# Gate and up projections of a SwiGLU FFN as 2x2 block products, three of eight K steps in Strassen's seven products (float32 in two halves, one core)

## The reference

```python
hf = rmsnorm(x, norm_ffn[l])
act = jax.nn.silu(jnp.einsum('bsd,df->bsf', hf, w_gate[l])) * jnp.einsum('bsd,df->bsf', hf, w_up[l])
x = x + jnp.einsum('bsf,fd->bsd', act, w_down[l])
return rmsnorm(x, norm_final)
```

## Time and profile before

| what | value |
|---|---|
| median of 3 runs | 1759.29 us (1758.98 to 1760.27) |
| profiled execution, span from its first to its last instruction | 1757.6 us |
| median of the runs over that span | 1.7 us |
| TensorE busy | 1745.9 us, 99% |
| VectorE busy | 862.1 us, 49% |
| ScalarE busy | 747.8 us, 43% |
| HBM read, mean rate | 328 MB, 188 GB/s |
| mean granted TensorE clock | 0.998 of full |

### The profile page before, as it was taken

The page is one execution under the profiler, slowest core; times in us unless marked ns, Lnnn a source line. Parts: engine busy times, 40 slices in busy tenths (PEclk is TensorE's granted clock), DMA queues, the critical chain, the costliest instruction groups (busy, mean ns, idle before and its releaser), DMA issues.

```text
span 1757.6 us, 20453 instructions
## 1 busy us (share of the span) xinstructions
PE 1745.9 (99%) x7883; PEld 1448.9 (82%) x7883; DVE 862.1 (49%) x652; ACT 747.8 (43%) x655; POOL 33.2 (2%) x43
## 2 busy tenths in 40 slices
PE   9999999999999999999999999999999999999997
PEld 8888888888888888888888888888888888888886
DVE  5454455556565444444445554444444444444445
ACT  6444444445454433333333443433333333444444
POOL 1000010100000000000000000000000000000000
PEclk9999999999999999999999999999999999999999
DMA  8656655556555655655556565555555555555552
GB/s 284 195 172 191 190 165 172 167 168 184 164 177 191 198 195 187 195 187 194 187 197 228 190 217 190 187 187 187 186 188 181 191 185 189 207 191 191 191 192 94
DMA packets 150699, 331.11 MB, mean 188 GB/s; under 512 B 7328, under 2 KB 7424, under 8 KB 144640
## 3 DMA queue, kind: packets, MB, share of 16 engines
q1 hardware_dynamic: 150656, 330.50, 57.1%
HBM read 328.38 MB, written 2.10 MB: 188 GB/s over the span
## 4 chain that ended last, share of the span: by engine, by line
PE 99%; ACT 0%; DVE 0%; DMA 0%; POOL 0%; SPq 0%; issue 0%; DVEq 0%; POOLq 0%
PE ps L1132 27%; PE ps L1133 27%; PE ps L1141 27%; PE ps L1408 4%; PE ps L1401 4%; PE ps L1403 4%; PE ps L1150 2%; ACT sq_y L738 0%; PE ps L1230 0%; PE ps L1222 0%; PE ps L1240 0%; PE ps L1247 0%; PE ps L1246 0%; PE ps L1239 0%; DMA vec_rows<-in_conv_w 0%; PE ps L1232 0%
## 5 line engine op out<-in xcount | busy, mean ns | idle before, releaser
L755 DVE TENSOR_TENSOR w_lo<-w_raw,w_hi 128x2048 fp32r<-128x2048 f32 x308 | 707.3, 2299 | 653.4 <-ACT w_hi L424 651.2
L424 ACT ACTIVATE w_hi<-w_raw 128x2048 fp32r<-128x2048 f32 (+1 forms) x309 | 589.7, 1912 | 515.2 <-PE ps L1133 366.5
L1132 PE MATMUL ps<-w_hi,xT_hi 128*128 128x512 f32 x1024 | 404.5, 395 | 0.0
L1133 PE MATMUL ps<-w_hi,xT_lo 128*128 128x512 f32 x1024 | 398.7, 389 | 0.0
L1132 PE MATMUL ps<-w_hi,fT_hi 128*128 128x512 f32 x704 | 274.9, 391 | 0.0
L1133 PE MATMUL ps<-w_hi,fT_lo 128*128 128x512 f32 x704 | 274.0, 389 | 0.0
L1141 PE MATMUL ps<-w_lo,xT_hi 128*128 128x512 f32 x1024 | 253.0, 389 | 0.0
L1132 PEld LDWEIGHTS ps<-w_hi,xT_hi 128*128 128x128 f32 x1024 | 192.3, 188 | 39.9 <-issue 0.2
L1141 PEld LDWEIGHTS ps<-w_lo,xT_hi 128*128 128x128 f32 x1024 | 192.2, 188 | 39.9
L1133 PEld LDWEIGHTS ps<-w_hi,xT_lo 128*128 128x128 f32 x1024 | 192.3, 188 | 39.0
L1141 PE MATMUL ps<-w_lo,fT_hi 128*128 128x512 f32 x704 | 173.9, 389 | 0.0
(11 more groups left out here) (179 smaller groups left out, 1039.1 us busy)
## 6 DMA issues: line engine op xcount, KB each, us to landing
w_raw<-in_w_in SPq DMA_DIRECT2D x127, 1024.0 KB, 5.5
w_raw<-in_w_gate SPq DMA_DIRECT2D x44, 1024.0 KB, 5.2
w_raw<-in_w_up SPq DMA_DIRECT2D x44, 1024.0 KB, 5.2
w_raw<-in_w_down SPq DMA_DIRECT2D x44, 1024.0 KB, 4.8
w_raw<-in_w_branch_a SPq DMA_DIRECT2D x16, 1024.0 KB, 5.1
w_raw<-in_w_branch_b SPq DMA_DIRECT2D x16, 1024.0 KB, 5.0
w_raw<-in_w_out SPq DMA_DIRECT2D x16, 1024.0 KB, 5.1
xn<-in_x SPq DMA_DIRECT2D x4, 512.0 KB, 8.4
```

Of the source, the lines that this page charges most:

```text
L424: copy = lambda o, i, **kw: nc.scalar.activation(o, i, ACT.Copy, **kw)
L755: V.tensor_tensor(w_lo[:, chunk.split, :], w_raw[:, chunk.raw, :], w_hi[:, chunk.split, :].bitcast(F32), ALU.subtract).then_inc(lo_split, 1)
L1132: T.matmul(ps[:, banks + r, :], rows(hi, k, r), w, start=(q == 0 and k == 0), stop=False)
L1133: last = T.matmul(ps[:, banks + r, :], rows(lo, k, r), w, start=False, stop=False)
```

## The change

The gate and the up block of one turn are taken as one problem of 2x2 blocks. The rows of A are the two row tiles (256 tokens), its columns the two halves of K (K tiles c and c+8); the columns of B are gate and up. A step now loads K tile c and K tile c+8 of both gate and up, two DMAs of 512 KB for one of 1 MB, in the order `PAIR_OF`. Five of the eight steps ("s" in `STEPS`) do the eight plain block products. Three ("S") do Strassen's seven: they need sums of the weight blocks and sums of the activation tiles. All go into seven PSUM banks whose contents VectorE adds up at the end of the turn; the plain steps use the same banks, with the difference A1 - A2 (`D1`, `D2`) where a bank's result is used in both rows.

In an S step VectorE makes three sums of weight blocks from `w_raw` (`t_raw`, one operation of 1024 columns, two of 512), ScalarE makes `t_hi` (1536 columns), VectorE makes `t_lo` (1536 columns), and then both split the loaded block as before. One of the four loaded blocks is overwritten by a sum in place. The sums of the activation tiles (`form_hi`, `form_lo`, 22 tiles) are made once, in the last block of the output projection (`forms(0)`) and in the first FFN turn (`forms(1)`); for them the transposed block goes to `f_raw` first. At the end of a turn VectorE does seven additions of 512 columns (`u_step`, `c_step`) where there were none, ScalarE copies one bank out (`p1_out`), and silu is two separate operations. The product is transposed in two halves, behind steps 1 and 2. The first and last step of a turn run bank by bank and want both halves of their weights at the start.

```diff
+STEPS = "SssSsSss"
+PAIR_OF = (0, 2, 3, 1, 5, 4, 6, 7)
+LAST_S = 5
+B_P1, B_P6, B_P2, B_Q3, B_Q4, B_FREE, B_P7, B_Q5 = range(8)
...
+            def load_pair(i):
+                for j in range(2 * BC):
+                    c = Chunk(G_FFN + j, i, 2 * BC)
+                    sp.wait_ge(lo_split, c.count(1 - RAW_SLOTS))
+                    for u, w in ((1, w_gate_k), (0, w_up_k)):
+                        sp.dma_start(raw_units[:, c.raw, :, u, :],
+                                     halves(w)[:, :, PAIR_OF[j], bass.ds(i * COLS, COLS)]).then_inc(
+                                         pair_landed[c.raw], 16)
...
+            def pair_split(j, i):
+
+                c = Chunk(G_FFN + j, i, 2 * BC)
+                if STEPS[j] == "s":
+                    split(c, (pair_landed[c.raw], 32 * (j // RAW_SLOTS + 1) + i * 64))
+                    return
+                before = S_BEFORE[j] + i * S_TURNS
+                act.wait_ge(t_step, before * T_STEPS + T_STEPS)
+                if not (starts(i) and j == 0):
+                    last = max(k for k in range(-2 * BC, j) if STEPS[k] == "S")
+                    act.wait_ge(lo_used, Chunk(G_FFN + last, i, 2 * BC).count(1))
+                copy(t_hi[:], t_raw[:].rearrange("p u n -> p (u n)")).then_inc(t_hi_done, 1)
+                split(c, (t_step, before * T_STEPS + T_STEPS))
...
+                    dve.wait_ge(t_lo_done, before)
+                V.tensor_tensor(t_raw[:, 0:2, :], raw[:, 0:1, :].to_broadcast([P, 2, COLS]), raw[:, 1:3, :],
+                                ALU.add).then_inc(t_step, 1)
+                dve.wait_ge(t_step, before * T_STEPS + 1)
+                V.tensor_tensor(raw[:, 0, :], t_raw[:, 0, :], raw[:, 2, :], ALU.add).then_inc(t_step, 1)
+                dve.wait_ge(t_step, before * T_STEPS + 2)
+                V.tensor_tensor(t_raw[:, 2, :], raw[:, 0, :], raw[:, 3, :], ALU.add).then_inc(t_step, 1)
+                dve.wait_ge(t_hi_done, before + 1)
+                V.tensor_tensor(t_lo[:], t_raw[:].rearrange("p u n -> p (u n)"), t_hi[:].bitcast(F32),
+                                ALU.subtract).then_inc(t_lo_done, 1)
+                split(c)
...
+                    if j == LAST_S:
+                        dve.wait_ge(p1_out, i + 1)
+                        if not first:
+                            dve.wait_ge(act_turned, i * 2)
+                        V.tensor_tensor(c_up[:, 0, :], ps[:, B_P6, :], c_gate[:, 0, :], ALU.add).then_inc(u_step, 1)
+                        dve.wait_ge(u_step, i * 2 + 1)
+                        V.tensor_tensor(c_gate[:, 1, :], ps[:, B_P7, :], c_up[:, 0, :], ALU.add).then_inc(u_step, 1)
...
+                add(1, c_gate[:, 0, :], B_P2, c_gate[:, 0, :], ALU.add)
+                dve.wait_ge(u_step, i * 2 + 2)
+                add(2, c_up[:, 0, :], B_Q5, c_up[:, 0, :], ALU.subtract)
+                add(2, c_up[:, 1, :], B_Q5, c_gate[:, 1, :], ALU.subtract)
+                dve.wait_ge(c_step, i * 5 + 2)
+                add(3, c_up[:, 0, :], B_Q3, c_up[:, 0, :], ALU.add)
+                add(4, c_gate[:, 1, :], B_Q4, c_gate[:, 1, :], ALU.add)
...
+            SUMS = ((B_P1, "A11", 1), (B_P6, "S2", 0), (B_P7, "D1", 5), (B_P2, "A12", 3), (B_Q5, "S1", 4),
+                    (B_Q3, "S4", 2), (B_Q4, "A22", 6))
+            PLAIN = ((B_P2, "A11", 1), (B_P2, "A12", 3), (B_Q5, "A21", 0), (B_Q5, "A22", 2),
+                     (B_Q3, "D1", 0), (B_Q3, "D2", 2), (B_Q4, "A21", 1), (B_Q4, "A22", 3))
...
+                if 0 < j < 2 * BC - 1:
+                    for part in parts:
+                        last = high(part, False)
+                    last.then_inc(hi_used, 1)
+                    pe.wait_ge(lo_split, c.count(1))
+                    for n, part in enumerate(parts):
+                        last = low(part, final(part[0]) and part[0] not in [p[0] for p in parts[n + 1:]])
+                    last.then_inc(lo_used, 1)
+                    return
+                pe.wait_ge(lo_split, c.count(1))
```

More of the change, by code:

```diff
@@ L276, in hybrid_block, with units @@
         GRP_HM, GRP_M, GRP_F = 0, NB, 2 * NB
-        HI_HM, HI_M, HI_F = 0, NB * KB, NB * KB + NB
+        HI_HM, HI_M = 0, NB * KB
+        S_TURNS = STEPS.count("S")
+        S_BEFORE = [STEPS[:j].count("S") for j in range(2 * BC)]
+        T_STEPS = 3
+        F_BLOCKS = NB - 1
+        def units(half):
+            w = w_hi if half == 0 else w_lo
+            return w[:].rearrange("p s (u n) -> p s u n", u=4)
         @block.sync
@@ L688, in ffn_turn, with silu @@
+            def silu(i, r):
+                if starts(i):
+                    act.wait_ge(x1_rstd, 1)
+                act.wait_ge(c_step, (1, 5)[r] + i * 5)
+                nc.scalar.activation(c_gate[:, r, :], c_gate[:, r, :], ACT.Silu,
+                                     scale=r_x[:, 1, r:r + 1]).then_inc(silu_done, 1)
+            def ffn_turn(i, last=False):
                 first = starts(i)
                 for j in range(2 * BC):
[L690 removed]
@@ L695, in ffn_turn @@
                         else:
[L696 to L701, removed]
-                            act.wait_ge(dve_out, V_FFN + i)
-                        for r in range(RT):
-                            last = nc.scalar.activation(gate[:, r, :], ps[:, r, :], ACT.Silu, scale=r_x[:, 1, r:r + 1])
-                        last.then_inc(act_out, 1)
+                            silu(i - 1, 1)
@@ new lines, in ffn_turn @@
+                    if not first and j in (1, 2):
+                        act_taken(i - 1, j - 1)
+                    if first and j == 2:
+                        forms_high(1, form_raw1, 12, 10)
+                    if j == LAST_S:
+                        act.wait_ge(lo_used, Chunk(G_FFN + j, i, 2 * BC).count(1))
+                        if not first:
+                            act.wait_ge(dve_out, V_FFN + i)
+                        copy(c_gate[:, 0, :], ps[:, B_P1, :]).then_inc(p1_out, 1)
@@ L708, in stage @@
+                    if last and j == LAST_S + 1:
+                        stage(Chunk(G_DOWN))
+                    if j == 2 * BC - 1:
+                        silu(i, 0)
             def stage(chunk):
@@ new lines, in ffn_turn, with add @@
+                    if last and j == LAST_S + 1:
+                        stage(Chunk(G_DOWN))
+                def add(n, out, bank, in1, op):
+                    if n < 4:
+                        dve.wait_ge(bank_done, i * 3 + n)
+                    else:
+                        dve.wait_ge(lo_used, Chunk(G_FFN + 2 * BC - 1, i, 2 * BC).count(1))
+                    V.tensor_tensor(out, ps[:, bank, :], in1, op).then_inc(c_step, 1)
+                add(1, c_gate[:, 0, :], B_P2, c_gate[:, 0, :], ALU.add)
@@ new lines, in turn_half, with turn_act @@
+            def turn_half(source, h, done):
+                for k in range(2):
+                    for r in range(RT):
+                        last = T.transpose(ps[:, B_FREE, k * SEQ + r * P:k * SEQ + (r + 1) * P],
+                                           source[:, r, (2 * h + k) * P:(2 * h + k + 1) * P], ident[:])
+                last.then_inc(done, 1)
+            def turn_act(d, h):
+                pe.wait_ge(dve_out, V_FFN + 1 + d)
+                if not (starts(d) and h == 0):
+                    pe.wait_ge(act_out_of, d * 2 + h)
+                turn_half(c_up, h, act_turned)
```

341 lines of the change are left out of this document (245 added, 96 removed).

## The result

The changed kernel takes **1813.4 us** (median of four runs, 1812.3 to 1814.3), the kernel before 1759.1 beside it: the ratio is 1.031, with a 95% interval of 1.0295 to 1.032. It is 54.3 us slower, where 1789.0 was forecast with a range up to 1813. In the experiments the kernel before ran beside each kernel again and took 1760.0 both times; ratios are to that, and differences between kernels of different occasions are good to about 1 us. The profiled execution took 1813.1 us, of which the span is 1811.3.

What follows compares the result with a forecast made beforehand. TensorE bounds the kernel before; VectorE's chain with serial `t_hi` copies would set the changed turn. -22.4 + 1.0 + 18.4 + 10 x 3.2 + 0.9 = +29.9 us, span 1757.6 to 1787.5, median 1789, range 1770 to 1813.

Steps and rivals of the forecast that it cites:

- The saving: TensorE's matmuls in the FFN: 99 fewer, -22.4 us, with 1.0 back for split transpositions: -21.4 us.
- The two cheap rivals: TensorE stays the bound within turns: 1757 us, chance 0.07; `t_hi` runs beside VectorE's other work: 1738 us, chance 0.05.
- the first rival: Clock falls to half in the new gaps, mainly at each turn's start: 1805 us, chance 0.25.
- A single fall, behind a tail with no work left: Argument against the clock falling in gaps: the trace before showed one fall, about 2.1 us behind the last matmul.
- half a step in half of the turns: Price of the clock's fall at step 0: 5.5 x 2.4 = 13 us, and some 3 at the start.
- A turn takes 45.6 us: One FFN turn under VectorE's chain: 1.2 us more than before, with 3.2 us of TensorE's waits.
- 4.4: Turn's start, from `w_lo` of step 0 done: VectorE's five additions and two products finish at 4.4 us.
- Hand-overs are short ... I take 0.05: Hand-overs between engines: 0.05 us each; 0.03 or 0.08 would move the total by -3 or +5.
- The timetable: One FFN turn, operation by operation from `w_lo` of step 0: TensorE waits 0.7 us before step 5, 2.5 before step 0.
- the paragraph before it: VectorE's turn: 37.8 us of work plus 4.8 behind `t_hi` makes 42.6, already TensorE's turn.
- What comes once: TensorE's waits from the output projection's last block through the first FFN turn: together 18.4 us.
- step 3's wait: First FFN turn: step 3's chain starts late behind the last transposed block's copies, TensorE waits 2.9 us.

Runs made afterwards that it cites:

- the second experiment: Changed kernel with VectorE's three weight sums of every S step put one split earlier, step 0's ahead of P1's additions (early sums): 1751.9 us, ratio 0.9952.
- the experiment with the fill: Changed kernel with ten idle matmuls ahead of the first step of turns 2 to 11: 1799.1 us, ratio 1.0223.
- The run with a third less of that work: Changed kernel with two S steps a turn in place of three, step 3 made plain: 1807.1 us, ratio 1.027.

## Why the prediction was right in kind and too low

**Right.** The saving: 99 matmuls, and with the waits gone (the second experiment) a turn of 42.44 us, where 42.5 was worked out. The durations: 1.76 and 1.49 from the middle between two neighbours gave 1.758 and 1.489. The place of the gaps: before step 0, released by `w_lo` (2.5 forecast, 2.6 measured), and before step 5, released by `w_hi` (0.7 and 0.75). The loads cost nothing: no wait of TensorE or VectorE in the FFN is put down to one. The two cheap rivals did not come, for the reason given: nothing stood between the sums and `t_lo` on VectorE. The second experiment put something there, and the turn became TensorE's own. VectorE's share was put at "about 85%" (37.8 of 45.6 us would be 83) and was 77.

**Wrong, first: the clock.** The step that failed is the weight of the first rival. It had the row for it: the clock was down 2.1 us after the last matmul, and the forecast itself had a gap of 2.5 us in each turn. "A single fall, behind a tail with no work left" was no argument against a number that was smaller than the gap. The rival should have been the forecast. Its price was well placed: "half a step in half of the turns", 13 us, against 14.4 between the two kernels. That is luck: the prediction had 2.4 us in 5.5 turns, and measured are some 1.47 in each of ten. Its way in was not the one written there (VectorE waiting for step 5), but ScalarE's wait for step 0's buffers.

**Wrong, second: the turn.** "A turn takes 45.6 us" was 46.40 without the clock's part. Three terms were short. "4.4" for the five additions and two products has no wait for `silu`, which stands on ScalarE (0.70 us) between the last addition and the second product and was among the terms costed at nothing: 0.23. `w_lo` of step 2 waits 0.30 for `w_hi`, which waits for TensorE's step 0. P1 comes 0.4 later behind `w_lo` of step 6 than forecast. Behind the last two stands "Hand-overs are short ... I take 0.05", read from two hand-overs. In the experiment with the fill ScalarE starts 0.12 us behind the sums (1341.05 to 1341.17) and TensorE 0.24 behind `w_lo` (1316.50 to 1316.74), and TensorE's first matmul behind a wait takes 0.1 longer to the next. What makes one hand-over longer than another is not shown; that the engine had been idle is not enough, for in the earlier trace rows VectorE had stood idle for 3.12 us and began after 0.03. With 0.1 won elsewhere the three terms make the 0.8 us, ten times over 8.0. The range allowed 5 for it.

**Wrong, third, and without effect on the sum: what sets the turn.** The timetable had the right waits, with the one exception told above, but the paragraph before it took VectorE's whole turn for the bound. The run with a third less of that work had the same turn. A stretch counts that begins and ends at TensorE: P1's copy, two additions, `w_lo`, three sums, `t_hi`, `t_lo`, `w_lo`.

**What comes once.** 18.4 us forecast, 15.0 measured as listed waits; the difference is in step 3's wait (2.9 and 0.9) for the most part. That is not what it cost, though. The second turn's first step starts 21.0 us later than before (1084.11 against 1063.10), where the forecast's terms give 18.9 (18.4, and the gap of 2.5, less 2.0 for nine matmuls). What gave the 3.4 us back and more was the half clock around the two longest waits (by the windows and my estimate 2.4 and 1.7 us) and the edges of six waits (0.3 each). Of the 24.4 us between 1789.0 and 1813.4, 8.0 are the turns, 14.7 the clock in them, and the 1.7 that are left go with these 2.1 us at the start.

## What to carry to other kernels

Where one engine makes another's operands through a third (sum, copy high, subtract low), put the first link one item ahead in the list before counting whether the work fits: the same instructions cost 61.5 us here by their order alone. Then ask which stretch starts and ends at the bounding engine, for only its length counts, and the next round's preparation belongs ahead of the wait for that engine's result (P1). Where TensorE must wait some 2.4 us or more in every round, count the clock's fall into the likeliest case, not into a rival (gaps of 1.8 us left it full here, and nothing in between was tried once a round); a few idle matmuls into a free bank cover what can't be removed.

## What the runs showed of the hardware

The clock falls inside a running kernel, behind one gap in 44 to 51 us of work: never at 1.7 to 1.8 us, in each turn at 2.4 to 2.6 us (some 1.5 us lost) and at 3.9 us (1.6 lost where the half clock lasted 3.4 us, 2.5 where it lasted 6.8). It does not have to fall within the gap. Behind a wait of 3.39 us in the changed kernel it fell 1.4 us after TensorE had started again, at 1043.67.

A gap's length alone doesn't decide, though. Around that wait of 3.39 us the clock fell in the changed kernel, and around the same wait it did not in the kernel with early sums, nor in the one with step 0's sums behind P1's additions; the first of these two had the half clock behind a wait of 1.86 us instead. Waits of 2.10 and 2.45 us in the changed kernel's first turn were not followed by a fall. What tells these apart stays open.

Ten idle matmuls in the gap kept it at full speed. A wait of TensorE costs 0.3 us more than it is listed with: turns with waits of 1.72 and 1.76 us were 2.03 and 2.01 longer than without. A matmul of 512 columns went in at 0.227 us from start to start, and at 0.42 to 0.43 on the half clock.
